# Attention's head norms: the squares split into a rounded part and the rest, summed by two one-pass products with ones

## What is computed

```python
DA_HEADS = 4
DA_V = 128
...
def rmsnorm(x, g):
    xf = x.astype(jnp.float32)
    y = xf * lax.rsqrt(jnp.mean(xf * xf, axis=-1, keepdims=True) + EPS)
    return (y * g.astype(jnp.float32)).astype(x.dtype)
...
    o = lax.map(block, (qb, jnp.arange(nb)))
    o = o.transpose(1, 0, 2, 3, 4).reshape(bsz, seq, nh, 2 * d)
    o = rmsnorm(o, sub_g) * (1.0 - lambda_init)
```

## Time and profile before

| | |
|---|---|
| three executions | 1314.1, 1314.4, 1315.09 us (median 1314.4) |
| span of the profiled execution, first to last instruction | 1310.8 us (3.6 us less than the median; its own time is not listed apart) |
| PE busy | 1290.9 us, 98% of the span |
| DVE, POOL, ACT busy | 849.4 us (65%), 637.2 us (49%), 493.5 us (38%) |
| the chain of work that ended last | PE 90%, DVE 5%, ACT 2%, POOL 2%, transfers 1% |
| granted PE clock | 1.00 over the span |

### The profile page before, as it was taken

How to read it: one execution, slowest core, us unless ns; L and a number is a source line. 1 busy time by engine, 2 the same in 40 slices (tenths; PEclk the granted TensorE clock), 3 DMA queues, 4 the chain that set the end, 5 groups by cost and what they waited for, 6 DMA issues and landing times.

```text
span 1310.8 us, 15989 instructions
## 1 busy us (share of the span) xinstructions
PE 1290.9 (98%) x6218; PEld 1054.8 (80%) x6218; DVE 849.4 (65%) x1142; ACT 493.5 (38%) x758; POOL 637.2 (49%) x302
## 2 busy tenths in 40 slices
PE   7999999999999999999999999999999999999999
PEld 4888886787888888888878888867878888888887
DVE  8789885846888117775237799677477761377720
ACT  6332556744223112223344245566432221122220
POOL 2986661144444444444468776512444444444442
PEclk9999999999999999999999999999999999999999
DMA  6232331123333323333232322301333233233332
GB/s 222 81 97 65 97 89 33 28 94 113 97 97 115 101 74 97 97 98 110 84 111 82 87 65 92 87 25 53 99 106 97 97 106 103 81 97 97 109 111 87
DMA packets 40939, 120.49 MB, mean 92 GB/s; under 512 B 6432, under 2 KB 10656, under 8 KB 40864
## 3 DMA queue, kind: packets, MB, share of 16 engines
q1 hardware_dynamic: 40864, 119.46, 29.3%
HBM read 114.20 MB, written 2.10 MB: 89 GB/s over the span
## 4 chain that ended last, share of the span: by engine, by line
PE 90%; DVE 5%; ACT 2%; POOL 2%; DMA 1%; issue 1%; SPq 0%; POOLq 0%; ACTq 0%
PE bank L504 26%; PE bank L517 26%; PE bank L509 25%; PE bank L718 3%; PE bank L506 1%; ACT G L1079 1%; PE bank L766 1%; DMA raw<-in_w_in 1%; POOL wl L362 1%; PE bank L663 1%; PE bank L755 1%; DVE G L1568 1%; PE bank L596 1%; PE bank L611 1%; DVE ssum L1196 1%; PE bank L745 1%
## 5 line engine op out<-in xcount | busy, mean ns | idle before, releaser
L362 POOL TENSOR_TENSOR wl<-raw,wh 128x1024 fp32r<-128x1024 f32 (+3 forms) x208 | 507.1, 2439 | 629.4 <-ACT wh L903 385.1
L903 ACT ACTIVATE wh<-raw 128x1024 fp32r<-128x1024 f32 (+3 forms) x208 | 218.6, 1052 | 267.3 <-PE bank L509 207.9
L504 PE MATMUL bank<-xl,wh 128*128 128x512 f32 x1088 | 282.4, 397 | 0.0
L517 PE MATMUL bank<-xh,wl 128*128 128x512 f32 x1088 | 271.1, 391 | 0.0
L509 PE MATMUL bank<-xh,wh 128*128 128x512 f32 x1056 | 261.0, 389 | 0.0
L504 PEld LDWEIGHTS bank<-xl,wh 128*128 128x128 f32 x1088 | 202.8, 188 | 48.2 <-issue 5.9
L517 PEld LDWEIGHTS bank<-xh,wl 128*128 128x128 f32 x1088 | 203.2, 188 | 41.7
L509 PEld LDWEIGHTS bank<-xh,wh 128*128 128x128 f32 x1056 | 198.3, 188 | 41.5
L1230 DVE TENSOR_TENSOR x<-x,bank 128x512 f32<-128x512 f32 x64 | 43.9, 685 | 228.5 <-PE bank L517 228.4
L504 PE MATMUL bank<-ml,wh 128*128 128x512 f32 x512 | 137.5, 395 | 0.0
L517 PE MATMUL bank<-mh,wl 128*128 128x512 f32 x512 | 127.5, 389 | 0.0
(11 more groups left out here) (304 smaller groups left out, 1357.8 us busy)
## 6 DMA issues: line engine op xcount, KB each, us to landing
raw<-in_w_gu SPq DMA_DIRECT2D x88, 512.0 KB, 3.5
raw<-in_w_in SPq DMA_DIRECT2D x52, 512.0 KB, 3.7
raw<-in_w_dn SPq DMA_DIRECT2D x32, 704.0 KB, 4.1
raw<-in_w_ol SPq DMA_DIRECT2D x16, 384.0 KB, 3.1
raw<-in_w_oe SPq DMA_DIRECT2D x16, 256.0 KB, 2.6
x<-in_x SPq DMA_DIRECT2D x8, 256.0 KB, 6.2
raw<-in_w_first SPq DMA_DIRECT2D x4, 512.0 KB, 3.8
out_x<-x SPq DMA_DIRECT2D x8, 256.0 KB, 4.6
```

The source lines that it names most:

```text
L362: tt(wl[:, p, 0:cols], raw[:, p, 0:cols], wh[:, p, 0:cols].bitcast(F32), ALU.subtract).then_inc(wl_full, 1)
L504: mm(bank[b][:, :], wh[:, p, k * P:(k + 1) * P], lo[:, k, :], start=(k == 0), stop=False)
L517: w = mm(bank[b][:, :], wl[:, p, k * P:(k + 1) * P], hi[:, k, :], start=False, stop=(k == K - 1))
L903: fn(wh[:, p, 0:cols], raw[:, p, 0:cols], ACT.Copy).then_inc(wh_full, 1)
```

## The change

ACT squares a head's output twice: into `xh[:, 0, :]`, which rounds to fp32r, and into `pad` as before. POOL subtracts the first from the second and leaves the rest in `xl[:, 0, :]`; `HEAD_LOW` says before which of the output units' `low` calls it does so (the fourth, sixth, seventh and ninth, counted from 0 as 3, 5, 6, 8). PE waits for POOL's rest in place of ACT's square, and sums with two one-pass products with `ones_r`, a copy of the matrix of ones in fp32r, which DVE makes once at the start of layer 0.

```diff
+HEAD_LOW = [3, 5, 6, 8]
...
+        ones_r = sb("ones_r", [P, P], F32R)
...
-                for _ in range(16 + 2 * (2 * FHALF + 8)):
+                for n in range(16 + 2 * (2 * FHALF + 8)):
+                    if n in HEAD_LOW:
+                        h = l * HEADS + HEAD_LOW.index(n)
+                        pool.wait_ge(osq_ready, h + 1)
+                        tt(xl[:, 0, :], pad[:, 0, 4:4 + T], xh[:, 0, :].bitcast(F32), ALU.subtract).then_inc(osq_low, 1)
                     low()
...
             def head_sum(b):
-                pe.wait_ge(osq_ready, nth(osq_ready))
+                pe.wait_ge(osq_low, nth(osq_low))
                 claim(b, head_ln)
-                mm(bank[b][:, :], ones, pad[:, 0, 4:4 + T], start=True, stop=True).then_inc(act_bank[b], 1)
+                mm(bank[b][:, :], ones_r[:, :], xh[:, 0, :], start=True, stop=False)
+                mm(bank[b][:, :], ones_r[:, :], xl[:, 0, :], start=False, stop=True).then_inc(act_bank[b], 1)
...
                 def head_square():
                     act.wait_ge(head_copied, nth(head_copied))
+                    fn(xh[:, 0, :], ssum[:, :], ACT.Square)
                     fn(pad[:, 0, 4:4 + T], ssum[:, :], ACT.Square).then_inc(osq_ready, 1)
...
                         copy(cbf[:, 0, :], ident)
+                        copy(ones_r[:, :], ones)
                         copy(block_r[:, :], block1).then_inc(block_ready, 1)
                         lambdas()
```

More of the change, by code:

```diff
@@ L238, in build @@
         token_ready = sem("token_ready")
-        head_copied, osq_ready, head_ln, onorm_done = [
-            sem(n) for n in ("head_copied", "osq_ready", "head_ln", "onorm_done")]
+        head_copied, osq_ready, osq_low, head_ln, onorm_done = [
+            sem(n) for n in ("head_copied", "osq_ready", "osq_low", "head_ln", "onorm_done")]
         g_ready, g_silu, h_ready, h_high, hid_ready = [
```

## The result

The changed kernel takes 1319.3 us (median of 6 executions, 1317.55 to 1319.71) against 1314.53 for the kernel before beside it. The medians differ by 4.8 us; the ratio on record is 1.0033 [1.0023, 1.0044], which is +4.3 us [3.0, 5.8]. It is slower, as forecast, but by 4.8 us and not by 3.2, and 1319.3 lies above the forecast's range of 1315.6 to 1318.8.

The account below looks back on a forecast made before the run. The prediction took PE, busy nearly without a break, to bound the kernel, with PE and DVE/ACT taking turns in the attention. Heads 1.9 plus cast 1.34 made 3.2 us, added to 1314.4: 1317.6 us, range 1315.6 to 1318.8.

Parts of the forecast that it names:

- Head 0: Head 0's sum: PE done at 232.07 instead of 231.98, then waiting 0.55 us for DVE anyway, so 0.
- Head 1: Head 1's sum: no wait, PE 0.40 us earlier, which becomes idle time at the wait for DVE at 255.65, so 0.
- The 2.58 us from square to sum: Every head: time from the first square's start to PE's start, through second square and POOL's subtraction, 2.58 us.
- POOL's 1.30: Every head: POOL's subtraction for the rest takes 1.30 us, read from the key norms.
- rival (c): POOL's subtraction slower beside DVE, 0.44 us more at heads 2 and 3 of both layers: 1319.4 us; chance 0.09.
- 2 x (0.08 + 0.86): The heads' cost over two layers: PE loses 0.08 us at head 2 and 0.86 at head 3, together 1.9 us.
- The new cast: Layer 0, before the decay products: POOL holds DVE's casts and products, lengthening PE's gap from 1.32 to 2.66 us, +1.34.
- Rival (a): The cast in layer 0 costs nothing, swallowed by the hold of `cbf<-pre`; only the heads lose: 1316.3 us; chance 0.30.
- The forecast's own two terms: The heads of both layers, 1.9 us, and the longer gap from the cast in layer 0, 1.34 us.
- the signs it named: In the profile: head 3's sum some 2.6 us after the square, the pair 0.46 us, layer 0's gap 2.66 us.
- The rival of the late first weights: Raised with the experiments: the later first weights belong to the change, first matmul at 9.57 us instead of 7.44; no chance given.

Follow-up runs that it names:

- e1: Kernel before plus DVE's unused cast of ones in the changed kernel's place; +1.5 us [0.7, 3.0] on the kernel before, median 1316.3 us in executions at full clock.
- e5: The changed kernel again, no edit, on another chip; +3.7 us [2.4, 5.3] on the kernel before.
- e4: Kernel before plus the unused cast of ones on DVE behind the decay rates' operations; +0.9 us [-0.4, 2.0] on the kernel before.
- e6: Kernel before plus the unused cast of ones in four pieces, giving a long PE gap; +3.4 us [2.4, 4.7] on the kernel before.
- e7: Kernel before with DVE's three casts (identity, block ones, mask) moved to ACT, heads unaltered; 1313.26 us against 1314.78, ratio 0.9988.
- e2: Changed kernel with the cast of ones on ACT instead of DVE; +1.5 us [0.7, 3.0] on the kernel before.
- e3: e2 with each layer's last head again using one square and one plain fp32 product; 0.0 us [-1.2, 1.2] on the kernel before.
- e8: e2 with the last head's rest subtracted by DVE instead of POOL; +0.9 us [-0.3, 2.1] on the kernel before.

## Why the prediction was wrong

**Right: the direction and its places.** The loss comes from head 3 and from the cast, and the shorter products earn nothing. Head 0: from its square to the wait for DVE's probabilities it is 238.73 - 233.82 = 4.91 us in the changed kernel's timeline and 233.94 - 229.03 = 4.91 before, so 0 as predicted:

```profile
233.82 0.63 ACT L1091 ACTIVATE xh<-ssum 128x512 fp32r<-128x512 f32 x1 [0.76 <-DVE ssum L1583]
...
238.73 0.66 PE L761 MATMUL bank<-cst,G 128*128 128x128 f32 x4 [0.54 <-DVE G L1576]
```

Head 1 doesn't wait, and what it saves turns up as a wait for DVE at 252.38. The amount, 0, is as predicted, the place is not: the same product starts at 247.59 in the kernel before (in both it is 18.56 us behind head 0's square), and the prediction had the wait at 255.65.

```profile
250.53 0.48 PE L780 MATMUL bank<-xh,ones_r 128*128 128x512 f32 x1
250.85 0.40 PE L781 MATMUL bank<-xl,ones_r 128*128 128x512 f32 x1
252.38 0.66 PE L761 MATMUL bank<-cst,G 128*128 128x128 f32 x4 [0.26 <-DVE G L1576]
```

**Right within 0.3 us: the heads.** The 2.58 us from square to sum were 2.56 (268.74 to 271.30), POOL's 1.30 was 1.27 without an outlier, so rival (c) falls. The pair holds PE for 0.57 us (271.30 to 271.87), not 0.46: its first product takes 0.33. Its weights begin to load at 271.30, together with it, while the load of the L702 of the earlier trace rows begins 0.23 us ahead of its product (143.33 and 143.56 in the timeline). The wait need not be the reason: head 1 doesn't wait, its load begins at 250.50, and its first product takes 0.32 as well. With that 2 x (0.08 + 0.86) became 2 x (0.16 + 0.95) = 2.2.

**Right within 0.2 us: the hold.** For the 1.34 us of "The new cast" the gap gave 1.14 here, 1.20 in e1 and 1.07 in e5. Rival (a), the cast swallowed, falls with e1.

**Wrong: what the gap costs.** The step that failed is the last one of "The new cast": "since PE is busy all the time after it, the 1.34 is never won back". It takes the price of the gap to be its length, and PE's speed behind it to be what it was. The earlier trace rows showed a clock of 1.00 behind a gap of 1.32 us, and I carried that over to a gap twice as long. In the changed kernel's profile the clock fell to 0.50, and PE lost another 1.61 us while busy. The prediction had no term, no bound and no rival for it. Rival (c) gives nearly the measured time, 1319.4, but by slow subtractions, and these took 1.27 us. The forecast's own two terms with their measured sizes, 1.14 + 2.22 = 3.4, are what e5's profile shows (+3.5), in an execution whose clock stayed up. That e5's median, 1318.5, lies inside the forecast's range is luck: the step lacks the clock there too, and in most of its executions the fall didn't come.

The price of 1.6 is that of the profiles. In the times it is blurred by their spread: the median of the changed kernel's four executions with a mean clock below 1.000 is 1319.5, that of the other two 1318.3, and in e1 it is 1317.1 against 1316.3.

**Wrong for the same reason: the signs it named.** The prediction's last part looks at the length of the gap and at waits. A loss in busy time is seen in neither; the windows' clock column, or the same instructions' time before and after, shows it.

The rival of the late first weights falls too. In ten profiles the mark lies between 18.40 and 20.93 us, and the profile of before is the earliest of all. The median time less the profile's length from the mark, an estimate of what lies outside it, is 22.4 us for before, 22.7 for e1, 22.5 for e4, 21.9 for e6 and 22.4 for e7, and with the heads' change 22.0 in the changed kernel, 21.8 in e2, 22.0 in e3, 22.6 in e5 and 22.3 in e8. So the kernels with the change don't start later than those without.

## What to carry to other kernels

Price a longer wait of PE by what follows it as well as by its length: look at the granted clock behind the gaps that the trace has, and treat a gap longer than any of these as a case of its own, with half speed for a while as the other end of the range. A one-time cast is not cheap because it is short: on DVE beside a busy POOL it cost this kernel 1.1 to 1.2 us, and on ACT (e2) the gap stayed at 1.28. Splitting an operand can pay only where the consumer comes later than the split is done, and isn't about to wait for something else: compare the distance between producer and consumer with the split's whole path, head by head, before counting PE time saved.

## What the runs showed of the hardware

The clock of PE fell to its lower level after a single idle stretch of 2.46 us in one profiled execution and not after stretches of 2.52 and 2.39 us in two others. By the mean clock it fell in each of the 10 executions of e6, whose profiled gap is 3.56 us, in 9 of the 24 of the three kernels with 2.4 to 2.5 us, and in none of the 44 of e2, e3, e4 and e8, with 2.18 us or less. After the fall it came back while PE was busy, and each fall that a profile shows cost 1.6 us (e6: 92.87 - 87.50 = 5.37 us for the instructions that took 3.73 before). What decides between the executions at 2.4 to 2.5 us is open; no run varied it.

In the changed kernel a DVE cast passes between two POOL instructions in its own 0.21 us (`ones_r` at 79.27, `cbf<-pre` at 80.61), and the next one of the same shape behind `ones_r` is held for 1.29. So the one short cast moved every later hold of this run by one place, and its own row shows nothing of the cost.
